# The end of a mixture-of-experts decoder step: PSUM copies of the running sums, joined statistics and stores, and one scatter behind the last weight column

## The reference, cut to what matters

```python
logits = (xt @ router_w).astype(f32) + router_b          # 16 experts, top 2 of one group of 4
...
for e in range(N_EXPERTS):
    h = jax.nn.silu(xt @ w_gate[e]) * (xt @ w_up[e])      # 2048 -> 1024
    y = y + combine[:, e:e + 1] * (h @ w_down[e])         # 1024 -> 2048
...
x = layer_norm(ALPHA * x + moe_ffn(x, ...), ln2_g, ln2_b)
# layer_norm: y = (x - mean) * rsqrt(var + 1e-5) * g + b, over the 2048 columns of each row
```

## Time and profile before

| | |
|---|---|
| time, median of 3 runs | 1657.43 us (1656.62 to 1657.88) |
| time of the profiled execution | 1656.72 us |
| its span in the profile | 1654.9 us |
| TensorE busy | 1592.7 us, 96% of the span |
| VectorE, ScalarE, GpSimd busy | 684.9, 391.0, 46.8 us |
| DMA in the 18 slices from 827 to 1572 us | 430 to 434 GB/s |
| DMA in the last slice (41.4 us) | 174 GB/s |
| the chain that ended last | TensorE 78%, DMA 19%, VectorE 1%, ScalarE 1% |

### The profile page before, as it was taken

How to read it: one execution, slowest core, us unless ns; L and a number is a source line. 1 busy time by engine, 2 the same in 40 slices (tenths; PEclk the granted TensorE clock), 3 DMA queues, 4 the chain that set the end, 5 groups by cost and what they waited for, 6 DMA issues and landing times.

```text
span 1654.9 us, 25151 instructions
## 1 busy us (share of the span) xinstructions
PE 1592.7 (96%) x11180; PEld 1060.0 (64%) x11180; DVE 684.9 (41%) x1030; ACT 391.0 (24%) x419; POOL 46.8 (3%) x85
## 2 busy tenths in 40 slices
PE   9999999999999999999999998998998899999998
PEld 9999999999999999973532523424334234225334
DVE  7437678657575665544520110111021011102726
ACT  7444555533453333320000000000000000000002
POOL 2000000022000000000000000000000000000000
PEclk9999999999999999999999999999999999999999
DMA  9676576589656769879999999999999999999995
GB/s 265 185 224 171 156 202 171 162 248 324 175 159 185 236 177 344 253 312 417 424 430 432 430 432 431 432 434 432 432 432 432 431 432 431 432 431 431 431 415 174
DMA packets 240709, 543.88 MB, mean 329 GB/s; under 512 B 5072, under 2 KB 218144, under 8 KB 227312
## 3 DMA queue, kind: packets, MB, share of 16 engines
q1 hardware_dynamic: 233536, 524.93, 83.4%
q0 software_dynamic: 4896, 15.49, 2.9%
q10 hardware_dynamic: 2192, 2.20, 0.4%
HBM read 535.65 MB, written 6.95 MB: 328 GB/s over the span
## 4 chain that ended last, share of the span: by engine, by line
PE 78%; DMA 19%; DVE 1%; ACT 1%; issue 0%; SPq 0%; DVEq 0%; ACTq 0%
PE bank L981 16%; PE bank L662 13%; PE bank L663 12%; PE bank L664 12%; PE bank L1075 10%; DMA ring_low<-wu 10%; DMA ring_high<-wu 8%; PE bank L944 5%; PE bank L1153 3%; DMA ring_low<-w_in 2%; PE bank L1109 1%; PE bank L1061 1%; PE bank L716 0%; PE bank L1147 0%; PE bank L998 0%
## 5 line engine op out<-in xcount | busy, mean ns | idle before, releaser
L664 PE MATMUL bank<-x_hi,w_lo 128*128 128x264 f32 x1216 | 344.8, 284 | 0.0
L662 PE MATMUL bank<-x_hi,w_hi 128*128 128x264 f32 x1200 | 344.2, 287 | 0.0
L663 PE MATMUL bank<-x_lo,w_hi 128*128 128x264 f32 x1200 | 340.5, 284 | 0.0
L981 PE MATMUL bank<-ring_low,reg_pk 128*64 128x512 f32 x1248 | 282.2, 606 | 25.3 <-DMA ring_low<-wu 25.3
L1456 DVE TENSOR_TENSOR w_lo<-ring_low,w_hi 128x2048 fp32r<-128x2048 f32 x107 | 244.8, 2289 | 137.2 <-ACT w_hi L1260 136.7
L1260 ACT CAST w_hi<-ring_low 128x2048 fp32r<-128x2048 f32 x107 | 203.8, 1904 | 141.6 <-PE bank L664 86.1
L664 PEld LDWEIGHTS bank<-x_hi,w_lo 128*128 128x128 f32 x1216 | 228.2, 188 | 0.0
L662 PEld LDWEIGHTS bank<-x_hi,w_hi 128*128 128x128 f32 x1200 | 226.6, 189 | 1.8 <-issue 1.3
L663 PEld LDWEIGHTS bank<-x_lo,w_hi 128*128 128x128 f32 x1200 | 226.4, 189 | 0.1
L981 PEld LDWEIGHTS bank<-ring_low,reg_pk 128*64 128x64 f32 x1248 | 88.6, 139 | 212.0 <-issue 171.7
L981 PE MATMUL bank<-ring_high,reg_pk 128*64 128x512 f32 x768 | 175.9, 613 | 22.8 <-DMA ring_high<-wu 20.8
(11 more groups left out here) (385 smaller groups left out, 1697.3 us busy)
## 6 DMA issues: line engine op xcount, KB each, us to landing
ring_high<-wd SPq DMA_DIRECT2D x21, 4096.0 KB, 30.0
ring_low<-wg SPq DMA_DIRECT2D x21, 4096.0 KB, 30.0
ring_low<-w_in SPq DMA_DIRECT2D x76, 1024.0 KB, 5.8
ring_high<-wu SPq DMA_DIRECT2D x14, 4096.0 KB, 23.0
ring_low<-wu SPq DMA_DIRECT2D x14, 4096.0 KB, 25.5
ring_low<-wd SPq DMA_DIRECT2D x7, 4096.0 KB, 31.6
ring_high<-wg SPq DMA_DIRECT2D x7, 4096.0 KB, 30.9
ring_low<-wo SPq DMA_DIRECT2D x16, 1024.0 KB, 7.2
```

Of the source, the lines that this page charges most:

```text
L662: pe.matmul(out, hi[k], of_hi[:, k, :], start=(k == 0), stop=False)
L663: pe.matmul(out, hi[k], of_lo[:, k, :], start=False, stop=False)
L664: mm = pe.matmul(out, lo[k], of_hi[:, k, :], start=False, stop=(k == kk - 1))
L981: mm = pe.matmul(psum[2 * a + part][64 * half:64 * half + 64, :], xg[:, k, CAP * a:CAP * a + CAP], wt[:, kk, 512 * half:512 * half + 512], ...
```

## The change

- **Loads.** In the middle pairs (1 to 6), units 18 and 19 (`ALONE`) come with a DMA each instead of one for both; in the last pair that holds for 14 to 19 (`LAST_SINGLE`). `unit` waits for the one unit alone there.
- **Gain.** `gain_out` is split: banks 0 and 1 right after unit 18's matmuls and the last `scatter_first`, banks 6 and 7 in `down_last`. ScalarE copies the first two after the first expert's result.
- **PSUM copies.** Before the transposes, two matmuls `identity x acc_s` put the sample rows' sums into banks 0 and 1; behind the transposes (now into bank 4), two matmuls `identity x acc` put columns 1536 to 2047 of both row tiles into banks 2 and 3. The scatters of the last column and of the sample rows accumulate onto them. `add_part` of the last column and `sample_add` are gone; statistics and gain read those banks.
- **Scatter.** `scatter_last(2)` moves from the middle of the last weight column to behind it. `out_part` is gone: ScalarE copies whole banks.
- **Norm.** The sample rows' statistics are passed as two sets of six numbers through four matmuls with `twins` (four shifted copies of the identity, made by GpSimd) and aggregated in one VectorE instruction. `quarter` is gone. The banks of `carried` and `shifted` change; the last column quarter of row tile 0 is also made by `carried` and `shifted` and scaled by ScalarE.
- **Stores.** Row tile 1 goes out in two DMAs of two blocks; block 3 of row tile 0 goes out from ScalarE's queue. Ten stores in all.

```diff
+LAST_SINGLE = 14
+ALONE = (18, 19)
...
-                for m in range(SINGLES if first else 0, UNITS - 4 if last else UNITS, 2):
+                for m in range(SINGLES if first else 0, LAST_SINGLE if last else UNITS, 2):
                     s = slot_of(m)
+                    if m in ALONE:
+                        for one in ALONE:
+                            sp.wait_ge(w_used, i * UNITS + (W_FREE + one - 7))
+                            sp.dma_start(ring_slot(slot_of(one)), weights(experts, one)).then_inc(landed[slot_of(one)], 16)
+                        continue
                     sp.wait_ge(w_used, i * UNITS + (W_FREE + m - 6))
                     sp.dma_start(two_slots(s), two_units(experts, m)).then_inc(both_landed[s // 2], 16)
+                for m in range(LAST_SINGLE, UNITS - 4) if last else ():
+                    sp.wait_ge(w_used, i * UNITS + (W_FREE + m - 7))
+                    sp.dma_start(ring_slot(slot_of(m)), weights(experts, m)).then_inc(landed[slot_of(m)], 16)
...
                         if last and a:
                             scatter_first(i, 4 * part + q - 1)
+                            if 4 * part + q == UNITS - 18:
+                                pe.wait_ge(rows_in, 16 * 8)
+                                gain_out((0, 1)).then_inc(gain_mm, 1)
...
-                gain_out().then_inc(gain_mm, 1)
+                gain_out((2, 3)).then_inc(gain_mm, 1)
+                pe.wait_ge(gain_ev, 2)
+                for half in range(2):
+                    pe.matmul(psum[half][:, 0:256], ident[:, :], acc_s[:, 256 * half:256 * half + 256], start=True, stop=False)
...
                 fill(1, psum[5])
-                hid_transposed(i, 1)
-                fill(2, psum[5])
+                hid_transposed(i, 1, 4)
+                for half in range(2):
+                    at_col = 1536 + 256 * half
+                    pe.matmul(psum[2 + half][:, :].rearrange("p (a n) -> p a n", n=256), ident[:, :], acc[:, :, at_col:at_col + 256], start=True, stop=False)
                 pe.wait_ge(hid_ev, i * 2 + 2)
...
-                        if c and k == 3:
+                        if 0 < c < 3 and k == 3:
                             scatter_last(i, c - 1)
                     mm.then_inc(w_used, 1)
+                scatter_last(i, 2)
                 scatter_last(i, 3)
...
-                            act.copy(ob[0:64, 256 * c:256 * c + 256], psum[4 + c % 2][0:64, 0:256]).then_inc(lob_act if c < 3 else ob_act, 1)
+                            act.copy(ob[:, 256 * c:256 * c + 256], psum[4 + c % 2][:, 0:256]).then_inc(lob_act if c < 3 else ob_act, 1)
```

More of the change, by code:

```diff
@@ L952, in gather, with unit @@
                     gather_part(p, r)
-            def unit(i, m, first=False, own=False):
+            def unit(i, m, first=False, own=False, last=False):
                 if first and m in once:
@@ L962, in unit @@
                 s = slot_of(m)
-                made = (1 if s >= 4 and not own else 0) + m // 8 + 1
+                if m in ALONE and not first:
+                    pe.wait_ge(landed[s], i * 16 + 48)
+                    return ring_slot(s)
+                if last and m >= LAST_SINGLE:
+                    pe.wait_ge(landed[s], 48)
+                    return ring_slot(s)
+                made = (1 if s >= 4 else 0) + m // 8 + 1
+                if own:
+                    made -= (1, 0, 1, 2)[s // 2]
+                doubles = 2 if s // 2 == 1 else 3
                 if first:
@@ L1117, in down_last @@
                         rows = slice(64 * half, 64 * half + 64)
-                        mm = pe.matmul(psum[4 + half][32 * nn:32 * nn + 32, 0:256], chosen[rows, 2 * P:2 * P + 32], ob[rows, 256 * nn:256 * nn + 256], start=True, stop=True)
+                        mm = pe.matmul(psum[half][32 * nn:32 * nn + 32, 0:256], chosen[rows, 2 * P:2 * P + 32], ob[rows, 256 * nn:256 * nn + 256], start=False, stop=True)
                 mm.then_inc(sc_mm, 1)
@@ L1195, in shifted, with sample_stats, carried @@
-            def shifted(tt, c):
+            def sample_stats():
+                pe.wait_ge(twin_ready, 1)
+                pe.wait_ge(s_part, 1)
+                for nn in range(4):
+                    mm = pe.matmul(psum[5][:, 12 * nn:12 * nn + 12], twins[:, nn, :, :].rearrange("p r x -> p (r x)"),
+                                   stat[:, 2, 0:2, :].rearrange("p n s -> p (n s)"), start=True, stop=True)
+                mm.then_inc(s_avg, 1)
+            def carried(tt, c, bank):
+                pe.matmul(psum[bank][:, :], ident[:, :], scaled_acc[:, tt, 512 * c:512 * c + 512], start=True, stop=False)
@@ L1197, in shifted @@
+            def shifted(tt, c, bank):
                 rows = slice(32 * c, 32 * c + 2)
-                pe.matmul(norm_bank(tt, c)[:, :], shift_rows[rows, P * tt:P * tt + P], ln2_rows[rows, :], start=(tt == 0), stop=True).then_inc(rank_two, 1)
+                pe.matmul(psum[bank][:, :], shift_rows[rows, P * tt:P * tt + P], ln2_rows[rows, :], start=(tt == 0 and c < 3), stop=True).then_inc(rank_two, 1)
             def last_norm(made):
-                carried(0, made + 2)
-                pe.wait_ge(sc_ev, (NPAIR - 1) * N_SC + 8)
@@ L1230, in _ @@
+                carried(0, 3, 7)
+                shifted(0, 3, 7)
             pe.wait_ge(plan_ready, 1)
@@ L1403, in pair @@
                             act.copy(ob[:, 0:512], psum[4][:, :]).then_inc(ob_act, 1)
+                            act.wait_ge(gain_mm, 1)
+                            for c in range(2):
+                                act.copy(ln2_gain[:, 512 * c:512 * c + 512], psum[c][:, :]).then_inc(gain_ev, 1)
                         else:
@@ L2050, in last_norm @@
-                link(dve.tensor_tensor(ms[:, 2:3], ms[:, 2:3], ms[:, 2:3], ALU.mult))
-                dve.tensor_tensor(ms[:, 1:2], ms[:, 1:2], ms[:, 2:3], ALU.add).then_inc(s_part, 1)
-                scaled(2, 7)
-                scaled(3, 4)
-                dve.wait_ge(s_avg, 2)
-                dve.tensor_copy(ms[:, 0:1], psum[0][:, 0:1])
-                dve.tensor_copy(ms[:, 1:2], psum[0][:, 1:2]).then_inc(l_var, 1)
+                for half in range(2):
+                    ins = dve.bn_stats(stat[:, 2, half, :], sample_half(half, own))
@@ L2057, in last_norm @@
+                ins.then_inc(s_part, 1)
+                for half in range(2):
+                    gain_last(half, own)
+                dve.wait_ge(s_avg, 1)
+                dve.bn_aggr(ms[:, 0:2], psum[5][:, 0:48]).then_inc(l_var, 1)
+                scaled(0, 1)
+                scaled(1, 3)
+                gain_part(0, 2)
                 dve.wait_ge(l_std, 3)
@@ L2059, in last_norm @@
                 dve.wait_ge(ln2q_in, 16 * 8)
-                link(dve.scalar_tensor_tensor(out=acc_s, in0=acc_s, scalar=ms[:, 0:1], in1=ln2q[:, 0, :], op0=ALU.subtract, op1=ALU.mult))
+                for half in range(2):
+                    cols = slice(256 * half, 256 * half + 256)
+                    ins = dve.scalar_tensor_tensor(out=acc_s[:, cols], in0=sample_half(half, own), scalar=ms[:, 0:1], in1=ln2q[:, 0, cols], op0=ALU.subtract, op1=ALU.mult)
+                link(ins)
                 dve.scalar_tensor_tensor(out=acc_s, in0=acc_s, scalar=ms[:, 3:4], in1=ln2q[:, 1, :], op0=ALU.mult, op1=ALU.add).then_inc(ys_ready, 1)
+                dve.wait_ge(xg_ready, made + 8)
+                scaled(2, 6)
             so_far = chain[0]
```

203 lines of the change are left out of this document (88 added, 115 removed).

## The result

The changed kernel takes 1667.37 us (median of 4 runs, 1666.3 to 1667.7) against 1657.26 us before: ratio 1.0059, 95% interval 1.0047 to 1.0072. It is slower by 0.6%, 10.1 us, where 3.7 were forecast. The profiled execution took 1667.14 us, its span is 1665.2 us, 10.3 more than before.

The account below looks back on a forecast made before the run. Bounds seen: DMA until 1489.86 us, then TensorE's instructions, then a 19 us end of short hand-overs. Terms -0.9 +0.9 +0.6 +1.0 -1.1 +0.65 +2.5 = +3.65 on 1657.43 gave 1661.1, stated as 1661.0; range 1657.3 to 1663.3.

Parts of the forecast that it names:

- Single loads: Seventh pair's end: unit 18 lands sooner, so TensorE's 0.93 us idle goes; gain between 0.9 and 1.7, taken as -0.9 us.
- Split gain: Two gain matmuls now stand in TensorE's unbroken stretch, where nothing hides them: between 0 and 1.1, taken as +0.9 us.
- Copies before and behind the transposes: Around the transposes: copies and filler lengthen the window before (+0.6 us), two 512-column copies outlast ScalarE's cover behind (+1.0 us).
- Third scatter moved: Last weight column: the scatter of 1.11 us leaves the columns and stands behind them, so they end earlier, -1.1 us.
- E to the aggregates: From the columns' end to the aggregates' end: saved add pays for four statistics, third column's work stands in line, +0.65 us.
- A: The moment the aggregates of the last norm end, from which the prediction counted the rest of the kernel.
- From the aggregates to the end: Last norm and stores: TensorE's serial matmuls, then ScalarE's scaling and three DMAs, set the end, +2.5 us (+1.0 to +3.5).
- the ten slots: TensorE's chain of carried and shifted matmuls in the last norm: ten at 0.86 us and run-out, 9.0 to 9.4 with changes.
- The rival with the clock: Last norm: granted clock falls after TensorE's wait and sparse matmuls, end at +5.3 us, 1662.8; chance 0.15.
- The changes between full-width and two-row matmuls: Last norm's chain: five changes of matmul kind, each costing up to 0.25 us more, of which half was taken.

Follow-up runs that it names:

- e1: Kernel before with only the change's single loads (18 and 19 in middle pairs, 14 to 19 in the last); 1654.62 us, ratio 0.9987.
- e10: Changed kernel without the four identity matmuls that copy running sums to PSUM, outputs not the reference's; 1666.55 us, ratio 1.0060.
- e7: e4 with each two-row matmul of the last norm replaced by one over all 128 rows, mean and bias term left out; 1660.97 us, one execution.
- e3: Kernel before without its five fillers ahead of the wait for shift_ready; 1657.51 us, ratio 1.0004.
- e8: Kernel before with the single loads and ScalarE copying whole banks of column results, VectorE's half copies gone; 1654.27 us, ratio 0.9983.
- e4: Changed kernel with 13 fillers instead of 8 ahead of the shift_ready wait and 5 instead of 1 ahead of the sample statistics; 1666.07 us, ratio 1.0056.
- e5: Changed kernel with the norm's last seven matmuls reordered, three full-width ones first, then four two-row ones on different row groups; 1662.42 us, ratio 1.0029.
- e9: e5 with block (0,3) combined by VectorE as in the kernel before, without its carried matmul and ScalarE scaling; 1662.54 us, ratio 1.0033.

## Why the prediction was wrong, by its steps

The direction held, the size didn't, and 1667.37 lies outside the range of 1657.3 to 1663.3.

- **Single loads, -0.9: -1.5 in the changed kernel, -1.3 alone (e1), counted from where unit 16 can start.** The mechanism, the limit at unit 6 and the range of 0.9 to 1.7 were right. I had taken the lower bound from the profiled execution, in which the clock fell in the batch before; in the executions of after and e1 it didn't.
- **Split gain, +0.9: +1.06.** Right.
- **Copies before and behind the transposes, +0.6 and +1.0: +0.76 and +0.92.** Right in the profile; e10 won 1.7 us at the columns' start by leaving them out, and its profile lost 1.1 of them in the chain at the low clock.
- **Third scatter moved, -1.1: -1.2. E to the aggregates, +0.65: +0.5.** Right. Up to A the sum of the forecast's terms was +1.15, that of the profile is +0.3.
- **From the aggregates to the end, +2.5: +10.0. This step failed.** The number of slots, their order and the hand-over to ScalarE were as I wrote them; 3.8 us from the last bank to the end, forecast 4.5. The first shifted matmul came at A + 3.2 (2.85 forecast), since VectorE's reciprocal began 1.05 us behind A, as before, where I had 0.4: the gain product that I thought delayed it had covered VectorE's reading of `pairs` (0.55 us) and the branch on it, which now stand open as idle time. But the ten slots took 16.8 us, not 9. I had priced each at the full clock.

```profile
1642.35 0.17 DVE L2057 RECIPROCAL small<-small 128x2 f32<-128x2 f32 x1 [0.85 <-ACT small L1444]
```

- **The rival with the clock** named the right mechanism and, in part, its place, and I gave it 0.15 and +1.7 us. Both were too small. I had read the price from a batch of matmuls over all 128 rows, in which the clock was back before the batch's end. Here it was down to the last matmul. Each lone slot behind the fall took 2.0 us instead of 0.9, and the ten together 16.8 here and 18.0 in e10: the term should have been some 8 to 9 us, not 1.7. With the clock held (e7, 1661.0, with one slot and nine fillers more than the change has, five of them in time that was idle, and fewer changes of kind) the forecast's 1661.0 would have been about right; that agreement is one execution's, and partly luck.
- **The trace of before had shown it.** Its own granted clock was 0.50 from 1648.5 on the earlier trace rows, right behind a stretch of two-row, one-column and a few full matmuls, in which TensorE was busy. I put it down to TensorE having stopped, at 1648.44, 0.1 us earlier. e1, e3 and e8 then showed the fall within work. That activity holds the clock up, as the prediction has it, was too coarse: TensorE counted as busy for 14.99 of 15.00 us at 0.50.
- **The changes between full-width and two-row matmuls** are six, not the five I counted. At the full clock a lone carried matmul between two-row ones took 1.05 us (e4, at 1648.82), all-row neighbours 0.86 each (e7). That is 0.2 for a change, where I had allowed 0.25 and taken half. The Trainium skill ("TensorEngine Tiling (Array Packing)", Key Properties) says that a change of tiling mode drains TensorE; the trace agrees in direction.

What stays open is how much of e5's gain is the returned clock and how much the row groups, since no run held one of them fixed; whether the low rows or the changes of kind count for more in the fall, since e7 took both away; and what decides the moment of the fall, which differs between executions of the same work.

## What to carry to other kernels

Price a chain near the end of a kernel at both clocks, and ask what holds the clock up there: here a busy TensorE wasn't enough, and fillers ahead of the chain didn't prevent the fall. Keep matmuls with few rows together, on different row groups, instead of alternating them with full-width ones; here an order alone took 5 of 10 us back. Where a DMA joins two units that are consumed one after the other, the join to split is the last one before a stretch bound by compute: TensorE waits there for both although it needs one, and splitting that join brought 1.3 us by the profiles here and cost nothing that could be seen.

## What the runs showed of the hardware that was not expected

- TensorE 100% busy with a granted clock of 0.50 for 15.0 us (after) and 17.7 us (e10, from 1643.1), in a mixture of two-row and full-width matmuls of 512 columns; with all of them over 128 rows the clock was 1.00 for the 9.7 us of the same chain (e7).
- The clock came back within such a chain when full-width matmuls stood in a row, three in e5 (0.50 until 1651.5, then 1.00) and two in e9 (until 1652.0), and fell again 0.6 and 1.4 us after TensorE's last matmul.
- Executions with the same work up to the chain had the fall 0.8 (e9), 1.8 (after) and 2.8 us (e5) behind the first shifted matmul.
- In e10 the fall came 0.3 us behind it, and the ten slots took 18.0 us, 1.1 more than in the changed kernel.
